# Token transform of the Fourier mixing: half of the output times computed, the other half written as mirror images

## The reference, cut to what matters

```python
def fourier_mix(u):
    B, T, _ = u.shape
    ug = u.reshape(B, T, FOURIER_GROUPS, FOURIER_GROUP_DIM).astype(jnp.float32)   # 4 groups of 256 features
    f = jnp.fft.fft2(ug, axes=(1, 3), norm='ortho').real
    return f.astype(u.dtype).reshape(B, T, FOURIER_WIDTH)
# layer 1
op  = fourier_mix(hp @ f_w_in[i]) @ f_w_out[i]     # context, T = 128
os_ = fourier_mix(hs @ f_w_in[i]) @ f_w_out[i]     # latent,  T = 256
```

## Time and profile before

| what | value |
|---|---|
| median of 3 runs | 815.8 us (814.9 to 817.2) |
| profiled execution | 817.36 us, of which the span is 815.5 us |
| PE busy | 778.3 us, 95% |
| PEld, DVE, ACT busy | 382.2, 335.8, 176.7 us |
| DMA | 277.44 MB, mean 340 GB/s |
| granted TensorE clock | 0.994 of full speed on average |

### The profile page before, as it was taken

How to read it: one execution, slowest core, us unless ns; L and a number is a source line. 1 busy time by engine, 2 the same in 40 slices (tenths; PEclk the granted TensorE clock), 3 DMA queues, 4 the chain that set the end, 5 groups by cost and what they waited for, 6 DMA issues and landing times.

```text
span 815.5 us, 10146 instructions
## 1 busy us (share of the span) xinstructions
PE 778.3 (95%) x3987; PEld 382.2 (47%) x3987; DVE 335.8 (41%) x750; ACT 176.7 (22%) x420; POOL 2.2 (0%) x9
## 2 busy tenths in 40 slices
PE   7899999999899999999978999999899999999986
PEld 3364545545444444444325657545444444444333
DVE  2216088225822644345307202225822644345316
ACT  3111566205411101110113401105411101110111
POOL 0000000000000000000000000000000000000000
PEclk9999999999999999999999999999999999999999
DMA  9979999924499999999999962024499999999993
GB/s 366 415 269 429 379 403 426 386 103 154 156 386 421 421 422 421 421 422 420 422 420 426 428 269 104 0 104 158 153 384 421 420 420 422 422 421 420 421 420 132
DMA packets 40050, 277.44 MB, mean 340 GB/s; under 512 B 8589, under 2 KB 9505, under 8 KB 11073
## 3 DMA queue, kind: packets, MB, share of 16 engines
q1 hardware_dynamic: 39649, 275.28, 82.4%
q10 hardware_dynamic: 288, 1.34, 0.4%
q0 software_dynamic: 64, 0.13, 0.0%
HBM read 275.04 MB, written 1.70 MB: 339 GB/s over the span
## 4 chain that ended last, share of the span: by engine, by line
PE 84%; DMA 7%; DVE 4%; ACT 2%; issue 1%; DVEq 1%; ACTq 0%; SPq 0%
PE bank L1881 24%; PE bank L1898 13%; PE bank L1779 10%; DMA ring<-in_moe_w 6%; PE bank L1866 6%; PE bank L1904 5%; PE bank L2273 4%; PE bank L1717 4%; PE bank L2136 4%; PE bank L2098 3%; PE bank L2294 1%; PE bank L2188 1%; PE bank L1759 1%; PE bank L1730 1%; PE bank L2209 1%
## 5 line engine op out<-in xcount | busy, mean ns | idle before, releaser
L1881 PE MATMUL bank<-ring,Z 128*64 128x512 f32 x1024 | 226.2, 594 | 8.4 <-DMA ring<-in_moe_w 5.6
L1881 PEld LDWEIGHTS bank<-ring,Z 128*64 128x64 f32 x1024 | 73.5, 137 | 145.8 <-issue 144.0
L1898 PE MATMUL bank<-ring,Z 128*64 128x512 f32 (+1 forms) x544 | 113.9, 570 | 0.7 <-DMA ring<-in_moe_w 0.7
L1779 PE MATMUL bank<-ring,T 128*128 128x512 f32 x192 | 83.1, 593 | 1.2 <-ACT T L1136 1.2
L1898 PEld LDWEIGHTS bank<-ring,Z 128*64 128x64 f32 x544 | 38.0, 137 | 68.5 <-issue 66.8
L1406 DVE TENSOR_TENSOR Z<-Z,bank 128x512 f32<-128x512 f32 x16 | 11.0, 688 | 134.9 <-PE bank L1881 134.9
L1779 PEld LDWEIGHTS bank<-ring,T 128*128 128x128 f32 x192 | 36.2, 190 | 45.6 <-issue 45.6
L1904 PE MATMUL bank<-ys,Cs 128*128 128x512 f32 (+1 forms) x204 | 52.3, 391 | 1.1 <-DVE ys L1423 1.1
L1436 DVE TENSOR_TENSOR x<-x,bank 128x512 f32<-128x512 f32 x84 | 52.0, 681 | 0.3
L1083 ACT ACTIVATE ys<-wg 128x512 fp32r<-128x512 f32 (+1 forms) x34 | 20.6, 605 | 136.1 <-DVE wg L1418 136.1
L1400 DVE COPY Z<-bank 128x512 f32<-128x512 f32 x24 | 16.6, 692 | 78.8 <-PE bank L1866 78.8
(11 more groups left out here) (237 smaller groups left out, 746.3 us busy)
## 6 DMA issues: line engine op xcount, KB each, us to landing
ring<-in_moe_w SPq DMA_DIRECT2D x192, 1024.0 KB, 15.8
ring<-in_ada_w SPq DMA_DIRECT2D x23, 2048.0 KB, 14.6
ring<-in_a_w_out SPq DMA_DIRECT2D x2, 2048.0 KB, 12.0
ring<-in_f_w_in SPq DMA_DIRECT2D x2, 2048.0 KB, 28.7
ring<-in_f_w_out SPq DMA_DIRECT2D x2, 2048.0 KB, 27.8
ring<-in_ada_w SPq DMA_DIRECT2D x2, 1024.0 KB, 8.4
ring<-in_a_w_in SPq DMA_DIRECT2D x4, 512.0 KB, 19.4
ring<-in_a_w_in SPq DMA_DIRECT2D x1, 2048.0 KB, 32.5
```

Source lines behind the costliest of these rows:

```text
L1779: last = pe.matmul(b[:, :], T[:, k, i * P:(i + 1) * P], w[:, k, :], start=(k == 0), stop=(k == KT - 1))
L1881: last = pe.matmul(out[BLK * u:BLK * (u + 1), :], xT[:, b, k, s0 + BLK * u:s0 + BLK * (u + 1)], w[:, k, :], start=(k == 0), stop=(k == KT ...
L1898: last = pe.matmul(end_banks[n][BLK * u:BLK * (u + 1), 0:e - a], aT[:, k, BLK * u:BLK * (u + 1)], w2[:, FC * hh + k, a - HALF * hh:e - HAL ...
```

## The change

The matrices of cosines and sines along time keep only the times 0 to T/2: 65 columns for the context (`CTX_T`) and 129 for the latents (`LAT_T`). TensorE's matmuls of the time transform produce 65 and 129 columns in place of 128 and 256. ScalarE copies the 194 columns of a sine bank to `uT[:, 2g+1, 0:194]`, whose old contents are no longer used. VectorE then writes both `T[:, 2g]` and `T[:, 2g+1]` from the cosine bank and this copy, in four pieces each: the context times 0 to 64, the context times 127 down to 65 (a destination with a step of -1), the latent times 0 to 128, and the latent times 255 down to 129. In mirrored pieces sum and difference change places. Nothing of it is written over, so `settle` is gone from this step. ScalarE writes the row of the middle frequency in the same four pieces. And TensorE waits at each k of the first output bank for what that k reads, no longer for three groups at once.

```diff
+CTX_T, LAT_T = SEQ // 2 + 1, DEC // 2 + 1
...
-    out["time_ctx"] = np.concatenate(dft(SEQ, SEQ ** -0.5), 1)
-    t = np.concatenate(dft(DEC, DEC ** -0.5), 1)
-    out["time_lat"] = t.reshape(2, P, 2 * DEC).transpose(1, 0, 2).reshape(P, -1)
+    out["time_ctx"] = np.concatenate([a[:, 0:CTX_T] for a in dft(SEQ, SEQ ** -0.5)], 1)
+    t = np.concatenate([a[:, 0:LAT_T] for a in dft(DEC, DEC ** -0.5)], 1)
+    out["time_lat"] = t.reshape(2, P, 2 * LAT_T).transpose(1, 0, 2).reshape(P, -1)
...
+        def times(half, row):
+            out = []
+            for at, n, first in ((0, SEQ, 0), (CTX_T, DEC, SEQ)):
+                out.append((half[:, at:at + n // 2 + 1], row[:, first:first + n // 2 + 1], False))
+                out.append((half[:, at + 1:at + n // 2], row[:, first + n - 1:first + n // 2:-1], True))
+            return out
...
                         act.wait_ge(dve_emptied, turn[("fT", 2 * g)][3])
-                        return act.activation(T[0:1, 2 * g + 1, :], middle[32 * g:32 * g + 1, 0:TOK], ACT.Copy)\
-                                  .then_inc(middle_out_done, 1)
+                        for half, row, _ in times(middle[32 * g:32 * g + 1, :], T[0:1, 2 * g + 1, :]):
+                            last = act.activation(row, half, ACT.Copy)
+                        last.then_inc(middle_out_done, 1)
...
                         b = stage_bank(("fT", 2 * g + 1), act)
-                        emptied_inc(act.activation(T[:, 2 * g + 1, :], b[:, 0:TOK], ACT.Copy))
+                        emptied_inc(act.activation(uT[:, 2 * g + 1, 0:CTX_T + LAT_T], b[:, 0:CTX_T + LAT_T], ACT.Copy))
...
-                halves_apart("fT", g, T, ALU.subtract, ALU.add)
+                b = stage_bank(("fT", 2 * g), dve)
+                dve.wait_ge(act_emptied, turn[("fT", 2 * g + 1)][3])
+                for f, ops in enumerate(((ALU.subtract, ALU.add), (ALU.add, ALU.subtract))):
+                    sines = [half for half, _, _ in times(uT[:, 2 * g + 1, :], T[:, 2 * g + f, :])]
+                    for (half, row, mirrored), sine in zip(times(b, T[:, 2 * g + f, :]), sines):
+                        last = dve.tensor_tensor(row, half, sine, ops[mirrored])
+                emptied_inc(last)
...
-                        if l == 1 and (hh, i) == (0, 0):
-                            done_by(("fT", KT - 4))
-                            pe.wait_ge(middle_out_done, FG - 1)
                         for k in range(KT):
-                            if l == 1 and (hh, i, k) == (0, 0, KT - 2):
-                                done_by(("fT", KT - 2), "fM")
+                            if l == 1 and (hh, i) == (0, 0):
+                                if k % 2 == 0:
+                                    done_by(("fT", k))
+                                else:
+                                    pe.wait_ge(middle_out_done, k // 2 + 1)
...
-                pe.matmul(out[:, 0:SEQ], v[:, 0, g, a:e], four("time_ctx")[:, part * SEQ:(part + 1) * SEQ],
+                pe.matmul(out[:, 0:CTX_T], v[:, 0, g, a:e], four("time_ctx")[:, part * CTX_T:(part + 1) * CTX_T],
                           start=True, stop=True, skip_group_check=True)
                 for q in range(2):
-                    last = pe.matmul(out[:, SEQ:TOK], v[:, 1 + q, g, a:e], tl[:, q, part, :],
+                    last = pe.matmul(out[:, CTX_T:CTX_T + LAT_T], v[:, 1 + q, g, a:e], tl[:, q, part, :],
                                      start=(q == 0), stop=(q == 1), skip_group_check=True)
```

## The result

The changed kernel takes 810.89 us (median of 5 runs, 810.43 to 812.85); before takes 815.8 (5 runs beside them, 814.69 to 817.2). The medians lie 4.9 us apart. The ratio estimated from all the runs is 0.9932, interval 0.9917 to 0.9947, which is a gain of 4.3 to 6.8 us. Run twice more beside the experiments the changed kernel gave 0.9926 (0.9903 to 0.9948) and 0.9934 (0.9914 to 0.9954).

What follows compares the result with a forecast made beforehand. TensorE, busy for 95% of the span, was taken to bound the kernel. Savings of 3.35 (banks), 0.75 (middle frequency) and 1.45 (gap), less 0.15, made 5.4 us: 810.4 us, own range 809.6 to 811.6.

Steps and rivals of the forecast that it cites:

- The banks: TensorE's eight banks of layer 1's time transform: 0.67 us each in place of 1.09, saving 3.35 us.
- The middle frequency: TensorE's row of the middle frequency, ahead of the eight banks: 1.1 us in place of 1.84, saving 0.75.
- The gap: TensorE's 1.45 us wait before layer 1's output projection goes whole, as VectorE and ScalarE have every input ready.
- cover at k = 7: In the first output bank, the last input is ready 3 us before TensorE wants it.
- Reaching the end: The 5.4 us reaches the kernel's end, since the expert weight transfers start with slots TensorE releases behind the change.
- Rival D: Expert stage gives the time back because the weight stream runs to its own clock: 815.8 us, chance 0.06.
- The range: Whole kernel: the forecast's own range, 809.6 to 811.6 us; with C and the scatter, 809.0 to 813.1.
- edges: From the middle frequency to the projection: 0.15 us for rounding and edges taken off the summed savings.
- the forecast: Whole kernel: 5.4 us saved, 810.4 us, chance 0.71.
- B: Time transform banks: no floor under a narrow pass, 0.55 us a bank, 1 us more saved, 809.4, chance 0.08.
- C: VectorE and ScalarE set the projection, at 2.64 us a group: gain 3.1 us, 812.7, chance 0.11.

Runs made afterwards that it cites:

- narrow: Changed kernel with 32 and 64 columns in a time transform matmul in place of 65 and 129, output wrong: 811.92 us, ratio to before 0.9943.
- wide: Changed kernel with 192 latent columns in each time transform matmul in place of 129, the rest unused: 811.0 us, ratio to before 0.9938.
- waits alone: Kernel before with only TensorE's waits changed, at each k of the first output bank for what it reads: 814.71 us, ratio 0.9974.
- doubled: Changed kernel with VectorE's four operations repeated into unused columns, sixteen a group in place of eight: 812.58 us, ratio to before 0.9939.
- old waits: Changed kernel with groups 0 to 2 awaited ahead of the first output bank, group 3 at k = 6: 812.73 us, ratio to before 0.9933.
- the pieces: Kernel before with VectorE's two operations a group each cut into four straight pieces, old full-length matmuls and waits kept: 816.1 us, ratio 0.9991.
- middle second: Changed kernel with group 0's two banks ahead of the middle frequency on TensorE: 810.14 us, ratio to before 0.991; again 809.83, 0.9916.

## Why the prediction was right

Predicted 810.4, measured 810.89, with 5.4 us forecast from the middle frequency to the projection and 5.52 seen. The mechanism in the stage is right. That the total is right to 0.5 us has luck in it: two things that were not forecast, 0.32 us won and 1.15 us given back, stand against each other.

- The banks: 0.67 us predicted, 0.67 measured; the narrow and the wide kernel show that a pass takes the larger of a floor of 0.11 us and the time of its columns. Reading the price from the feature transform, which has the same weights and almost the same widths, was what made this exact.
- The middle frequency: 1.1 predicted, 1.00 measured.
- The gap: gone, as predicted, and shown by the two kernels with the waits alone changed. That VectorE and ScalarE keep up was right with room: 1.34 us a group (1.4 predicted), 0.63 to 0.65 a middle row (0.7 to 0.8), 3.2 us of cover at k = 7 (3 predicted). The doubled kernel shows what happens when the cover is used up. By the Trainium skill, VectorE: DVE Perf Modes, section "The TRN2 errata — SBUF-src ops pay a fixed extra latency per instruction", a group would take 1.8 us (an estimate from its fixed cost for each instruction); the trace has 1.34. The eight pieces of a group last 2.0 us if their durations are added up, so they overlap, and the measurement decides.
- Reaching the end: right for the mechanism (nothing of the 5.9 us is lost between projection and experts, TensorE's waits for weights are 6.1 us after and 6.3 before), but 1.15 us was given back in the expert stage by another way, the clock, which the prediction did not price. Rival D had such a loss, of the whole gain and by the stream of weights; neither is what happened. Stage 5.52, first bank 0.07, the stretch to the experts 0.32 (last section), less 1.15 by the clock make 4.76; the medians say 4.9.
- The range: the bounds that the prediction names, 2.7 to 4.3 us for the banks and 0.4 to 0.9 for the middle frequency, with 1.45 for the gap and 0.15 less for edges, add up to 4.4 to 6.5 us, so 809.3 to 811.4 and not 809.6 to 811.6. And the chances of the forecast, B and C add up to 0.90, not 0.89. The result lies in either range.

**The clock in the expert stage.** TensorE of the changed kernel waits for weights, then takes 8.78 us for 32 matmuls; below it the same place before:

```profile
779.62 8.78 PE L1899 MATMUL bank<-ring,Z 128*64 128x512 f32 x32 [2.36 <-DMA ring<-in_moe_w]
```

```profile
786.99 7.09 PE L1881 MATMUL bank<-ring,Z 128*64 128x512 f32 x32 [2.37 <-DMA ring<-in_moe_w]
```

In the stretch 781.50 to 785.00 the changed kernel's granted clock is 0.65, a part of it at 1.2 GHz:

```profile
781.50:785.00 3.50, 3.50 (x14) 1.28 (x12) 0.00 (x0) 0.00 (x0) 0.00 (x0) 0.65 1.02 424
```

The wait is the same 2.4 us. It is followed by the fall in all three traces of the changed kernel and in the narrow one (expert products 220.8 to 221.1), and by none in before, the waits alone, the old waits, the doubled, the wide, the pieces and the two with the middle second (219.6 to 220.1). The 1.7 us of slower matmuls are partly paid by a wait that is gone (0.70 for L1898 before). The length of this wait alone does not decide it: it is 2.36 to 2.39 us in the four traces with the fall, and 2.36 to 2.63 in the eight without. Where in time the wait falls may decide, but no kernel was run that moves the wait alone, so the cause of the fall stays open. So does the question whether the change brings it about: all three traces of the changed kernel have it, while the doubled and the old waits, which differ from it by edits in this stage alone, do not.

## What to carry to other kernels

Price a narrower matmul from a stage of the same kernel with the same weight shape, and look for the floor: here a float32 pass with 128 x 128 weights took 0.11 us at 32, 64, 65 and 129 columns alike. When a step reads several pieces, wait for each where it is read; that alone was a quarter of what was won in stage and bank. And when the runs scatter by more than the effect, compare stages of traces, which repeated to 0.02 us here up to the experts, and look at the granted clock before believing a total.

## What was not expected of the hardware

VectorE stands still for a moment in the routing of layer 1 of the kernel before, with nothing to wait for; the waits of VectorE in the stretch before the experts say (total us, times, longest):

```profile
DVE PC L1322 <- issue: 0.2, 1, 0.2
```

and in the kernel in pieces, which has 24 more VectorE instructions ahead of it, at another line:

```profile
DVE h L1183 <- issue: 0.4, 1, 0.4
```

The changed kernel has neither, and its stretch to the experts is 60.29 us against 60.61 and 60.45. The waits alone, which leave VectorE's instructions as they are, keep the stall at L1322 and 60.59 us. That it reaches TensorE is seen in TensorE's waits for the product of L1339, first of the kernel before, then of the changed one, where that line is L1351:

```profile
PE bank L1827 <- DVE Ms L1339: 2.8, 2, 1.5
```

```profile
PE bank L1845 <- DVE Ms L1351: 2.4, 2, 1.2
```

The longest of these waits is 0.3 us shorter, which is nearly all of the 0.32. So in the kernel before the stall delays TensorE.

Its place goes by the number of VectorE's instructions ahead of it, not by their kind. If every instruction that the trace has of VectorE is counted, drains among them, the stall stands at the 773rd in the kernel before (L1322), in the waits alone (L1322) and in pieces (L1183). The doubled kernel has stalls of 0.4 us at the 901st (L1272, at 583.3, when the expert products have begun) and at the 1029th, and before and the waits alone have one of 0.4 at the 1029th too: 128 and 256 further on. It does not stand at each of these places in each kernel; the changed kernel has its 773rd at L1202 and no idle time there. Depending on where it falls it costs 0.3 us, 0.16 or nothing. What the engine waits for there was not shown.
